# Attention computed by pairs of heads: probabilities divided before they are turned, values as the stationary operand, result produced already transposed

## The chip, the cores and the metric

The kernel runs on one core of a Trainium2 chip. It is one program in which five engines work beside each other: PE (the matrix engine, TensorE), ACT (ScalarE), DVE (VectorE), POOL (GpSimd) and SP (SyncE, which here only issues the weight transfers). They hand work to each other through counters (semaphores). The metric is the device time of one execution in microseconds, the median of several runs; lower is better.

## The reference

Two transformer blocks of two layers each run on one sequence of 256 positions, model width 1024, in fp32. Three of the four layer mixers that matter here are attention, and each is followed by an output projection of width 1024:

```python
# "a": 12 heads of 64, three dilated bands mixed by their log-sum-exps (12*64 + 256 gated columns go into w_out)
scores = einsum(q, k) * dh ** -0.5; scores = where(valid, scores, NEG_INF)
# "c": 8 heads with 96 columns in q and k, 64 in v, and 8 grouped heads of 64 (8 query heads on 2 key heads)
p = softmax(einsum('bqkgc,bskc->bkgqs', q, k) * scale, axis=-1)
out = einsum('bkgqs,bskc->bqkgc', p, v)
# "s": 8 heads of 64 with a relative bias, a causal window and one sink logit per head,
#      beside a depthwise convolution of 31 taps, whose 512 columns form the other half of w_out's input
probs = softmax(concatenate([scores + bias, sink], -1), -1)[..., :-1]
```

Between the mixers lie mixtures of experts and dense feed-forward layers, which take most of the time and which the change does not touch. In "a" the three bands are computed as one softmax, whose mask carries the logarithm of how many bands hold a key.

## The kernel before

T = 256 positions lie in NT = 2 tiles of P = 128 partitions. The three attentions are made by three functions, one for each engine: `attend_pe` (L742), `attend_act` (L775) and `attend_dve` (L795). They walk through the heads in a hand-written software pipeline. For each head:

- PE makes the scores, two matmuls that stream 256 columns each (L751), into bank 4 or 5. The queries are the stationary operand. Heads of 64 columns lie by twos in the upper and lower 64 partitions of `qkA`, `dT` and `qkS` (`half_rows`), so an even and an odd head use different row halves of the array. The heads of 96 columns use 96 rows each.
- DVE scales the scores and adds the mask or bias (L807; L804 where there is none) into `probs`, then takes the row maxima (L809). For "s" two small steps bring in the sink (L814, L816).
- ACT takes the exponential of each of the two query tiles and sums the rows in passing (L784).
- PE turns the four 128x128 blocks by an ordinary fp32 matmul against the identity (L761) into bank 6 or 7, and ACT copies them to `probsT` (L793).
- PE multiplies them by the values, with a `probsT` block as the stationary operand and 64 value columns streaming (L771, four matmuls), into bank 2 or 3. DVE takes reciprocals of the sums (L825) and divides on the way into `cat` (L828).

PE's order for head i is: scores of i, turn of i-2, values of i-3. After the last head, all of `cat` (positions in the partitions) is turned by PE in transpose mode (`turn_pe`, L359, stages "cat_a", "cat_c", "cat_s", four groups each). ACT copies each group to `hT_hi` in the reduced format fp32r (L391), and DVE makes the rest `cat_lo` (L393) (`split_evac`). The output projection (`split_proj_pe`, L556, L576, L582) then multiplies both parts by weights which ACT and DVE have split in the same way (`unit_hi` L451, `unit_lo` L456), one unit of two 128-row blocks at a time. It starts when the first turned group and the first split unit are there.

What stands around the three attentions:

- "a": PE first makes the gating product (L918), and DVE takes it out (L891), before the first head.
- "c": the projections and turns of q and k come before it.
- "s": DVE also has the convolution's taps (L1485), two after each step of the head loop. After the attention the convolution is turned by PE (L1423), normalised by DVE (L1506 to L1519), passed through the silu by ACT (L1455), and turned again.

SP streams the weights through a ring of six 2 MB slots; a slot is loaded again when the engines release it.

## Time and profile before

| | |
|---|---|
| Runs | 1895.82, 1898.30, 1898.87 us; median 1898.3 us |
| Profiled execution, its span | 1897.7 us, mean granted clock of PE 0.898 |
| Busy: PE, ACT, DVE | 1606.0, 594.1, 886.1 us |
| "a": first scores to first matmul of the output projection | 91.15 to 157.46 us |
| "c": the same | 504.86 to 555.23 us |
| "s": the same | 1111.20 to 1164.64 us |

In the profile a row of the timeline is a run of like instructions: its start, how long it lasts, the engine, the line and the operands, and in brackets the idle time before it. An ordinary fp32 matmul has two records in the trace, so "x8" at L751, L761 or L771 is four matmuls; a transpose has one. The granted clock is written as a share of 2.4 GHz: 1.00 is the higher level and 0.50 is 1.2 GHz.

### The profile page before, as it was taken

Reading aid. Unit: us, or ns where it says so; the run is one execution under the profiler, and the core shown is the slowest. Engines: PE = TensorE matmul, PEld = TensorE weight load, DVE = VectorE, ACT = ScalarE, POOL = GpSimd, SP = SyncE. Lnnn points to the kernel's source line nnn. Section 1 sums busy time; section 2 is a strip of 40 time slices with the busy share of each in tenths; the row PEclk is TensorE's granted clock in tenths of the full one; section 3 lists DMA queues with packets and bytes.
Section 4 is the critical chain, followed back from the end, with each engine's and each line's share of the span. In section 5 each row is a group of like instructions: output and inputs, shape, how many; then the busy total and the mean of one; then the engine's idle time right before and its main releaser. Section 6 shows DMA issues by size and latency. Waiting matters only on the chain.

```text
span 1897.7 us, 27096 instructions
## 1 busy us (share of the span) xinstructions
PE 1606.0 (85%) x11040; PEld 1309.3 (69%) x11040; DVE 886.1 (47%) x1503; ACT 594.1 (31%) x952; POOL 25.2 (1%) x32
## 2 busy tenths in 40 slices
PE   7898766657796865659998988999989998879998
PEld 6787533226585422239998667899989997769997
DVE  5534311105763201145555576655565555475555
ACT  4333100004351100033443033443444442443442
POOL 0000000000100000000000000000000000000000
PEclk9858898788897978889999968999999998989999
DMA  9402499998112999995444422355545543345520
GB/s 405 195 0 89 202 426 428 428 428 344 46 45 73 427 429 428 429 407 206 182 177 179 134 89 83 139 182 185 196 166 195 184 178 129 124 170 206 181 89 22
DMA packets 31024, 409.24 MB, mean 216 GB/s; under 512 B 3376, under 2 KB 5424, under 8 KB 6368
## 3 DMA queue, kind: packets, MB, share of 16 engines
q1 hardware_dynamic: 28496, 404.85, 53.9%
q10 hardware_dynamic: 2448, 3.24, 0.6%
q8 instruction: 60, 0.98, 0.2%
q14 instruction: 20, 0.16, 0.0%
HBM read 407.01 MB, written 1.06 MB: 215 GB/s over the span
## 4 chain that ended last, share of the span: by engine, by line
PE 61%; DMA 17%; issue 12%; DVE 6%; ACT 3%; POOL 1%; SPq 0%; DVEq 0%; ACTq 0%; POOLq 0%
DMA ring<-stream 17%; PE bank L1267 7%; PE bank L1271 7%; PE bank L1268 7%; PE bank L1299 6%; PE bank L576 5%; PE bank L1305 3%; PE bank L751 3%; PE bank L761 3%; PE bank L582 2%; PE bank L1095 2%; PE bank L1541 2%; PE bank L771 2%; PE bank L1076 2%; PE bank L556 2%
## 5 line engine op out<-in xcount | busy, mean ns | idle before, releaser
L456 DVE TENSOR_TENSOR unit_lo<-ring,unit_hi 128x1024 fp32r<-128x1024 f32 x324 | 395.5, 1225 | 348.2 <-ACT unit_hi L451 347.9
L451 ACT ACTIVATE unit_hi<-ring 128x1024 fp32r<-128x1024 f32 x324 | 342.3, 1061 | 472.0 <-PE bank L1271 293.9
L1267 PE MATMUL bank<-hT_hi,unit_hi 128*128 128x256 f32 x1408 | 348.4, 286 | 0.4
L1268 PE MATMUL bank<-norm_lo,unit_hi 128*128 128x256 f32 x1408 | 346.6, 281 | 0.0
L1268 PEld LDWEIGHTS bank<-norm_lo,unit_hi 128*128 128x128 f32 x1408 | 266.6, 189 | 3.1
L1267 PEld LDWEIGHTS bank<-hT_hi,unit_hi 128*128 128x128 f32 x1408 | 265.6, 189 | 4.6 <-DVE norm_lo L395 1.4
L1076 PE MATMUL bank<-ring,work 128*32 128x256 f32 x2048 | 150.9, 451 | 90.9 <-DMA ring<-stream 77.7
L1271 PE MATMUL bank<-hT_hi,unit_lo 128*128 128x256 f32 x1408 | 197.6, 282 | 0.0
L1076 PEld LDWEIGHTS bank<-ring,work 128*32 128x32 f32 x2048 | 72.7, 126 | 167.8 <-DMA ring<-stream 100.3
L1271 PEld LDWEIGHTS bank<-hT_hi,unit_lo 128*128 128x128 f32 x1408 | 181.1, 189 | 0.0
L1299 PE MATMUL bank<-unit_hi,act_lo 128*128 128x512 f32 x336 | 132.4, 394 | 0.0
L1299 PE MATMUL bank<-unit_hi,act_hi 128*128 128x512 f32 x336 | 132.0, 393 | 0.0
L1219 DVE TENSOR_TENSOR work<-work,bank 128x128 f32<-128x128 f32 x32 | 9.2, 288 | 211.1 <-ACT work L1148 211.1
L1095 PE MATMUL bank<-ring,work 128*32 128x256 f32 x1024 | 79.2, 461 | 26.6 <-DMA ring<-stream 20.9
L359 PE MATMUL bank<-con,xn 128*128 128x128 f32 (+1 forms) x184 | 39.7, 404 | 61.6 <-ACT xn L678 61.6
L1305 PE MATMUL bank<-unit_lo,act_hi 128*128 128x512 f32 x336 | 90.1, 390 | 0.0
L1148 ACT ACTIVATE work<-bank 128x128 f32<-128x128 f32 x32 | 8.9, 278 | 248.9 <-PE bank L1076 248.9
L359 PEld LDWEIGHTS bank<-con,xn 128*128 128x128 f32 (+1 forms) x184 | 35.4, 214 | 66.3 <-ACT xn L678 56.7
L1095 PEld LDWEIGHTS bank<-ring,work 128*32 128x32 f32 x1024 | 39.2, 127 | 53.8 <-issue 27.0
L576 PE MATMUL bank<-unit_hi,hT_hi 128*128 128x512 f32 (+1 forms) x192 | 73.6, 389 | 1.4 <-ACT unit_hi L451 1.4
L1305 PEld LDWEIGHTS bank<-unit_lo,act_hi 128*128 128x128 f32 x336 | 63.1, 188 | 14.1
L1227 DVE COPY work<-bank 32x256 f32<-32x256 f32 x64 | 27.2, 424 | 97.8 <-PE bank L1095 97.3
(238 smaller groups left out, 2029.6 us busy)
## 6 DMA issues: line engine op xcount, KB each, us to landing
ring<-stream SPq DMA_DIRECT2D x191, 2048.0 KB, 14.4
work<-spread ACTq DMA_DIRECT2D x2, 1024.0 KB, 7.6
par<-params SPq DMA_DIRECT2D x1, 1451.5 KB, 17.5
x<-x_in SPq DMA_DIRECT2D x1, 1024.0 KB, 5.0
out<-x SPq DMA_DIRECT2D x2, 512.0 KB, 2.7
con<-consts SPq DMA_DIRECT2D x1, 640.0 KB, 5.9
cat<-final_rows ACTq DMA_DIRECT2D x1, 512.0 KB, 3.9
work<-final_rows ACTq DMA_DIRECT2D x1, 512.0 KB, 5.1
```

Of the source, the lines that this page charges most:

```text
L359: last = nc.tensor.transpose(bank[g % 4][0:rows, at:at + cols], src, ident)
L451: nc.scalar.activation(high_buf(name, u), raw_unit(name, u), ACT.Copy).then_inc(hi_done, 1)
L456: low = nc.vector.tensor_tensor(low_buf(name, u), raw_unit(name, u), high_buf(name, u).bitcast(F32), ALU.subtract)
L576: nc.tensor.matmul(proj_bank(m, t)[:, 0:width], left[:, 2 * j + kk, t * P:(t + 1) * P], high[:, kk, 0:width], start=(j == 0 and kk == 0 an ...
L751: mm = nc.tensor.matmul(bank[4 + g % 2][:, t * T:(t + 1) * T], q[:, t * P:(t + 1) * P], k, start=True, stop=True)
L1076: mm = nc.tensor.matmul(bank[4 + e % 2][32 * j:32 * j + 32, 0:256], hcur[:, 4 * half + kk, e * CAP:(e + 1) * CAP], w[:, kk, :, j * P:(j + ...
L1095: mm = nc.tensor.matmul(bank[7][32 * i:32 * i + 32, 0:256], actT_e[:, e % 2, j * CAP:(j + 1) * CAP], w[:, j, i * 256:(i + 1) * 256], start ...
L1267: nc.tensor.matmul(out, high[:, k, :], hT_hi[:, k, :], start=(k == 0), stop=False)
L1268: nc.tensor.matmul(out, high[:, k, :], norm_lo[:, k, :], start=False, stop=False)
L1271: mm = nc.tensor.matmul(out, low[:, k, :], hT_hi[:, k, :], start=False, stop=(k == KD - 1))
L1299: nc.tensor.matmul(bank[j][:, :], left[:, f % 2, t * P:(t + 1) * P], unit_hi[:, u % SPLIT, half * 512:(half + 1) * 512], start=(f == 0 and ...
L1305: mm = nc.tensor.matmul(bank[j][:, :], act_hi[:, f % 2, t * P:(t + 1) * P], unit_lo[:, u % SPLIT, half * 512:(half + 1) * 512], start=Fals ...
```

## The change

Heads are handled by twos. The scores of both go out in turn, tile by tile, into two banks. Where there is a mask or bias, DVE adds it and finds the maximum in one instruction for each half head; where there is none it only reads the maximum out of PSUM, and the exponential reads PSUM and scales. DVE divides the probabilities before they are turned. PE turns them in transpose mode, and then the values are the stationary operand (64 columns: the even head writes partitions 0 to 63, the odd one 64 to 127) with 256 turned probabilities streaming. The product is thus the transposed result, which ACT and DVE split straight into `hT_hi` and `cat_lo`. The turns of `cat` fall away, except for the two blocks of gated columns in "a" (group 3, now made right after the first scores, with PE waiting for its evacuation) and the convolution's half in "s". The convolution's turn now waits for all heads. The mask table, the bias and the sink table are prepared to fit.

```diff
+        def scores_pe(pe, name, i):
+            g, heads = PAIR_AT[name] + i, HEADS[name][2 * i:2 * i + 2]
+            ge(pe, probs_done, g - 1)
+            for t in range(NT):
+                for hh, (q, k, *_) in enumerate(heads):
+                    mm = nc.tensor.matmul(score_bank(g, hh)[:, t * T:(t + 1) * T], q[:, t * P:(t + 1) * P], k,
+                                          start=True, stop=True)
+            mm.then_inc(scores_done, 1)
+        def turn_probs_pe(pe, name, i):
+            pe.wait_ge(norm_done, g + 1)
+            for hh in range(2):
+                ge(pe, probsT_done, 2 * g - 1 + hh)
+                for s in range(NT):
                     for t in range(NT):
-                            mm = nc.tensor.matmul(bank[6 + g % 2][:, s * T + t * P:s * T + (t + 1) * P],
-                                                  probs[:, g % 3, t * T + s * P:t * T + (s + 1) * P], ident,
-                                                  start=True, stop=True)
+                        mm = nc.tensor.transpose(bank[hh][:, s * T + t * P:s * T + (t + 1) * P],
+                                                 probs[:, g % 3, hh, t * T + s * P:t * T + (s + 1) * P], ident)
+                mm.then_inc(probs_turned, 1)
+        def weigh_pe(pe, name, i):
+            ge(pe, cat_low, g - 1)
+            for s in range(NT):
+                for hh in range(2):
+                    if s == 0:
+                        pe.wait_ge(probsT_done, 2 * g + hh + 1)
+                    at = hh * NT * T + s * T
+                    mm = nc.tensor.matmul(bank[2 + g % 2][64 * hh:64 * hh + 64, 0:T], heads[hh][2](s),
+                                          PROBS_T[name][:, g % 2, at:at + T], start=(s == 0), stop=(s == NT - 1),
+                                          skip_group_check=True)
+            mm.then_inc(heads_done, 1)
+        def attend_pe(pe, name, between=None):
+            n = PAIRS[name]
+            scores_pe(pe, name, 0)
+            scores_pe(pe, name, 1)
+            if between is not None:
+                between()
+            for i in range(n):
+                if i >= 1 and i + 1 < n:
+                    scores_pe(pe, name, i + 1)
+                turn_probs_pe(pe, name, i)
+                if i >= 1:
+                    weigh_pe(pe, name, i - 1)
+            weigh_pe(pe, name, n - 1)
+        def attend_act(act, name, between=None):
+            for i in range(n):
+                exp_act(act, name, i)
+                if i == 0 and between is not None:
+                    between()
+                if i >= 1:
+                    probsT_act(act, name, i - 1)
                 if i >= 2:
+                    heads_hi_act(act, name, i - 2)
+            probsT_act(act, name, n - 1)
+            heads_hi_act(act, name, n - 2)
+            heads_hi_act(act, name, n - 1)
+        def masked_dve(v, name, i):
+            v.wait_ge(scores_done, g + 1)
+            for hh, head in enumerate(heads):
+                if head[4] is None:
+                    last = nc.vector.tensor_reduce(top[:, 2 * hh:2 * hh + 2],
+                                                   score_bank(g, hh)[:, :].rearrange("p (t s) -> p t s", t=NT), AX.X,
+                                                   ALU.max)
+                    continue
+                for t in range(NT):
+                    last = nc.vector.tensor_tensor_reduce(probs[:, g % 3, hh, t * T:(t + 1) * T],
+                                                          score_bank(g, hh)[:, t * T:(t + 1) * T], head[4](t), head[3], OFF,
+                                                          ALU.add, ALU.max, top[:, c:c + 1])
+        def norm_probs_dve(v, name, i):
+            v.wait_ge(probs_done, g + 1)
+            step(v, nc.vector.reciprocal(rsum, sums))
+            for hh in range(2):
+                for t in range(NT):
+                    last = nc.vector.tensor_scalar(row, row, rsum[:, c:c + 1], None, ALU.mult)
+            last.then_inc(norm_done, 1)
+        def heads_lo_dve(v, name, i):
+            v.wait_ge(cat_hi, g + 1)
+            nc.vector.tensor_tensor(cat_lo[:, i, :], bank[2 + g % 2][:, 0:T], hT_hi[:, i, :].bitcast(F32),
+                                    ALU.subtract).then_inc(cat_low, 1)
+        def attend_dve(v, name, between=None, first=None):
+            masked_dve(v, name, 0)
+            masked_dve(v, name, 1)
+            if first is not None:
+                first()
+            for i in range(n):
+                norm_probs_dve(v, name, i)
+                if i >= 1 and i + 1 < n:
+                    masked_dve(v, name, i + 1)
+                if i >= 2:
+                    heads_lo_dve(v, name, i - 2)
                 if between is not None:
                     between(i)
+            heads_lo_dve(v, name, n - 2)
+            heads_lo_dve(v, name, n - 1)
...
-            attend_dve(v, "a")
+            attend_dve(v, "a", first=lambda: split_evac(v, 1, "cat_a", 3))
-            attend_act(act, "a")
+            attend_act(act, "a", lambda: split_evac(act, 0, "cat_a", 3))
-            attend_pe(pe, "a")
-            pe.wait_ge(turn_src, 2)
-            pe.wait_ge(cat_done, HEAD_AT["a"] + A_HEADS)
-            turn_pe(pe, "cat_a")
+            def gated_turn():
+                pe.wait_ge(turn_src, 2)
+                turn_pe(pe, "cat_a")
+                pe.wait_ge(*TURN_DONE[TURN_AT["cat_a"][0]])
+            attend_pe(pe, "a", gated_turn)
...
             attend_pe(pe, "c")
-            pe.wait_ge(cat_done, HEAD_AT["c"] + C_HEADS + G_HEADS)
-            turn_pe(pe, "cat_c")
...
             attend_pe(pe, "s")
             pe.wait_ge(conv_done, 1)
+            pe.wait_ge(cat_low, PAIR_AT["s"] + PAIRS["s"])
...
-            pe.wait_ge(cat_done, HEAD_AT["s"] + S_HEADS)
-            turn_pe(pe, "cat_s", 0, 2)
             pe.wait_ge(conv_cat, 1)
-            turn_pe(pe, "cat_s", 2, 4)
+            turn_pe(pe, "cat_s")
...
-            attend_dve(v, "s", lambda i: taps(104 + 2 * i, min(106 + 2 * i, 4 * KW)))
+            attend_dve(v, "s", lambda i: taps(104 + 5 * i, 109 + 5 * i))
```

The new ACT functions: `exp_act` waits for the pair's maxima and makes four exponentials of 256 columns (and the sink's for "s"); `probsT_act` copies each head's 512 turned columns as soon as they are there; `heads_hi_act` makes `hT_hi` from 256 columns of the product.

## Rows read from the trace of the kernel before

**Rows 1.** By stretch: busy us of PE, PEld, DVE, ACT, POOL; clock, DMA, GB/s
```profile
130.00:140.00 10.00, 10.00 (x37) 8.09 (x36) 2.39 (x7) 3.15 (x10) 0.00 (x0) 0.50 0.00 0
499.00:502.00 3.00, 3.00 (x15) 2.81 (x15) 1.53 (x6) 0.65 (x2) 0.00 (x0) 0.50 0.03 5
502.00:504.80 2.80, 2.07 (x19) 1.80 (x17) 1.89 (x6) 1.98 (x7) 0.00 (x0) 0.99 0.00 0
523.00:547.00 24.00, 24.00 (x163) 20.35 (x163) 14.14 (x34) 12.72 (x41) 0.00 (x0) 1.00 0.00 1
1120.00:1145.00 25.00, 25.00 (x90) 20.44 (x89) 14.96 (x42) 8.33 (x30) 0.00 (x0) 0.50 0.00 1
```

**Rows 2.** Timeline of PE in "a": start us, us, line, operands, count
```profile
91.15 2.09 PE L751 MATMUL bank<-work 64*128 64x256 f32 x8
...
98.73 2.07 PE L751 MATMUL bank<-work 64*128 64x256 f32 x4
100.73 2.07 PE L761 MATMUL bank<-con,work 128*128 128x128 f32 x8
...
152.48 1.96 PE L771 MATMUL bank<-work 128*128 128x64 f32 x16
...
157.46 0.47 PE L576 MATMUL bank<-unit_hi,hT_hi 128*128 128x512 f32 x1 [0.59 <-ACT unit_hi L451]
```

**Rows 3.** Timeline of PE in "c" and the turns before it
```profile
498.80 3.52 PE L359 MATMUL bank<-con,work 128*96 128x128 f32 x16 [2.81 <-DVE xn L982]
502.16 1.91 PE L359 MATMUL bank<-con,xn 128*96 128x128 f32 x16
504.86 1.97 PE L751 MATMUL bank<-work 96*128 96x256 f32 x8 [0.79 <-DVE work L373]
...
550.38 1.96 PE L771 MATMUL bank<-work 128*128 128x64 f32 x16
...
555.23 0.47 PE L576 MATMUL bank<-unit_hi,hT_hi 128*128 128x512 f32 x1 [0.47 <-ACT unit_hi L451]
```

**Rows 4.** Timeline of PE in "s" and at its projection
```profile
1111.20 2.08 PE L751 MATMUL bank<-work 64*128 64x256 f32 x8 [5.37 <-issue]
...
1151.54 1.96 PE L771 MATMUL bank<-work 128*128 128x64 f32 x16
...
1164.64 0.78 PE L576 MATMUL bank<-unit_hi,hT_hi 128*128 128x512 f32 x1
...
1168.90 0.39 PE L576 MATMUL bank<-unit_hi,hT_hi 128*128 128x512 f32 x1
```

**Rows 5.** DVE's instructions by line and shape: busy, mean ns, idle before
```profile
L393 DVE TENSOR_TENSOR cat_lo<-bank,hT_hi 128x256 fp32r<-128x256 f32 x24 | 9.0, 418 | 2.9 <-ACT hT_hi L391 2.9
L688 DVE CUSTOM_DVE_ANT_0 xn<-x 128x1024 f32<-128x1024 f32 x12 | 14.7, 1225 | 5.0 <-DMA x<-x_in 4.6
L688 DVE DVE_READ_ACCUMULATOR2_ANT stat<- 128x1 f32 x12 | 1.0, 82 | 0.0
L809 DVE TENSOR_REDUCE stat<-work 128x2 f32<-128x512 f32 x36 | 24.7, 686 | 1.2
L1658 DVE TENSOR_SCALAR work<-work,stat 128x256 f32<-128x256 f32 x8 | 2.2, 349 | 17.9 <-ACT work L1594 17.9
L1485 DVE SCALAR_TENSOR_TENSOR cat<-work,par,cat 128x256 f32<-128x256 f32 x120 | 48.6, 478 | 0.0
```

**Rows 6.** Timeline of ACT in "a"
```profile
107.89 0.51 ACT L784 ACTIVATE work<-work,stat 128x256 f32<-128x256 f32 x1 [4.04 <-DVE stat L809]
...
108.40 0.49 ACT L784 ACTIVATE work<-work,stat 128x256 f32<-128x256 f32 x1
...
108.89 0.57 ACT L793 ACTIVATE work<-bank 128x512 f32<-128x512 f32 x1
```

**Rows 7.** ACT's splitting of a weight unit, by line
```profile
L451 ACT ACTIVATE unit_hi<-ring 128x1024 fp32r<-128x1024 f32 x324 | 342.3, 1061 | 472.0 <-PE bank L1271 293.9 <-PE bank L1305 114.4 <-PE bank L582 58.2
```

**Rows 8.** Timeline of PE, an expert's matmuls on 32-column strips of the array
```profile
211.12 3.66 PE L1076 MATMUL bank<-ring,work 128*32 128x256 f32 x64 [1.26 <-issue]
```

More of the change, by code:

```diff
@@ new lines, in build, with pair_stat, score_bank @@
+        PAIRS = {name: len(heads) // 2 for name, heads in HEADS.items()}
+        PAIR_AT = {"a": 0, "c": PAIRS["a"], "s": PAIRS["a"] + PAIRS["c"]}
+        SINK_NEG = 216
+        def pair_stat(g, what):
+            at = 20 * (g % 3) + 4 * ("top", "sums", "sink", "sink_exp", "rsum").index(what)
+            return stat[:, at:at + 4]
+        def score_bank(g, hh):
+            return bank[4 + 2 * (g % 2) + hh]
+        def scores_pe(pe, name, i):
[6 more added lines that the diff above has]
+            mm.then_inc(scores_done, 1)
@@ new lines, in attend_pe, with exp_act @@
+        def attend_pe(pe, name, between=None):
[11 more added lines that the diff above has]
+            weigh_pe(pe, name, n - 1)
+        def exp_act(act, name, i):
+            g, heads = PAIR_AT[name] + i, HEADS[name][2 * i:2 * i + 2]
+            act.wait_ge(masked_done, g + 1)
+            top, sums = pair_stat(g, "top"), pair_stat(g, "sums")
+            for hh, head in enumerate(heads):
+                for t in range(NT):
+                    row, c = probs[:, g % 3, hh, t * T:(t + 1) * T], 2 * hh + t
+                    masked = head[4] is not None
+                    src = row if masked else score_bank(g, hh)[:, t * T:(t + 1) * T]
+                    last = nc.scalar.activation(row, src, ACT.Exp, bias=top[:, c:c + 1], scale=1.0 if masked else head[3],
+                                                accum_out=sums[:, c:c + 1])
+            if name == "s":
+                last = nc.scalar.activation(pair_stat(g, "sink_exp"), pair_stat(g, "sink"), ACT.Exp)
+            last.then_inc(probs_done, 1)
```

172 lines of the change are left out of this document (68 added, 104 removed).

## Prediction

> **What bounds the kernel now.** I read the busy time by stretch first, because the page's averages mix the attention with stages that the change leaves alone. In the middle of each attention PE is busy all the time (10.00 of 10.00 us in "a", 24.00 of 24.00 in "c", 25.00 of 25.00 in "s"), while DVE has 2.4, 14.1 and 15.0 us of work in them and ACT 3.2, 12.7 and 8.3 [rows 1]. So PE sets the pace. It does so at two speeds: the granted clock is 0.50 in "a" and "s" (1.2 GHz) and 1.00 in "c" (2.4 GHz) [rows 1]. No weights move in these stretches (0 or 1 GB/s) [rows 1]: the ring is full, and what the attention saves no transfer takes back. The timelines then give the length of each stage. In "a" the last product ends at 152.48 + 1.96 = 154.44, 63.3 us after the first scores, and the projection starts 3.0 us later [rows 2]. In "c" these are 552.34, 47.5 us and 2.9 us [rows 3]; in "s" 1153.50, 42.3 us and 11.1 us, the last for the convolution's normalising and turns [rows 4].
>
> **PE's work for a pair.** Scores: in "a" the first two heads stood together in PE's queue. Their four matmuls took 2.09 us, and later the two of one head alone 2.07 [rows 2]. So heads in different row halves run at once, and the pair costs 2.1 us at the low clock instead of 4.1, and about 1.1 at the high one. The 96-column heads don't overlap: four matmuls took 1.97 at the high clock [rows 3]; I take 1.85 in a stream, and 3.6 at the low clock. Turns: a head's four matmuls against the identity took 2.07 at the low clock [rows 2], while 16 transposes took 3.52 at the low and 1.91 at the high one [rows 3], 0.22 and 0.12 each. Eight cost 1.95 and 1.1 with their start, instead of about 4.0 and 2.1. Values: before, two heads cost about 1.96 us at the high clock (the rows hold 16 records, so two heads) [rows 2 to 4]. Now there are four matmuls of 256 columns, with 64 stationary columns each, in two halves of the array. The trace has no such shape. The nearest is the experts' 32-column strips: 32 matmuls of 256 columns in 3.66 us, 0.11 each [rows 8], against 0.49 for one alone [rows 3], so four strips run at once. If two halves do the same, the pair costs 1.05 and 1.95 (high, low clock); if not, 1.9 and 3.6. I take the first, as the nearer row. In sum a pair costs PE 3.25 us at the high clock (4.0 with 96 columns) and 6.0 at the low (7.5), where "a" took 63.3/6 = 10.5 and "c" 47.5/8 = 5.9.
>
> **DVE and ACT: a new ring.** DVE divides pair i before it masks pair i+1, ACT can only then exponentiate i+1, and DVE waits for that to divide it. The three steps are in series and become the pace wherever PE is faster.
> - Divide: four multiplications of 256 columns at 2.2/8 = 0.275 [rows 5], with an allowance of 0.3 for the reciprocal and the hand-over inside DVE: 1.4 us.
> - Mask, "a": the fused instruction is only there for 1024 columns, 1225 ns and 82 for reading the maximum [rows 5]. A 256-column subtraction occupies 9.0/24 = 0.375 [rows 5]. So four cost 4 x 0.46 = 1.8 to 1.3 (if it scales by length alone, 4 x 0.39 = 1.55); with 0.2 for the sign I take 1.95. "c" only reads the maximum, 2 x 0.69 [rows 5] and 0.2: 1.55. "s": 2.25 with the sink's steps.
> - Exponentials: 0.50 from one to the next [rows 6]: 2.0 us; 2.1 reading PSUM, 2.2 with the sink.
>
> With 0.05 for each of three hand-overs the ring turns in 5.5 us in "a", 5.2 in "c", and 6.0 in "s", plus what the five taps (5 x 48.6/120 = 2.0 us [rows 5]) stick out behind the exponential, 0.2 to 0.4.
>
> **The three stages.** "a", high clock: the first scores wait for the gating columns to be taken out; masks of pairs 0 and 1 end at 5.2. The group of gated columns is copied by ACT and DVE by 6.8 (two copies of 256 columns each, PE waiting behind it with nothing else to do), pairs 0 and 1 are divided at 9.6 and pair 2 at 16.0, then three turns of the ring at 5.45 give 32.3, and the last transposes and two products 3.2: 35.5 us against 63.3. At the low clock pair 2 is divided at 18.8, PE's 6.0 sets the pace up to 36.8, and the end costs 3 x 1.95: 42.6. I take 38: low at the start as now, then PE has an unbroken row of full-width work and I expect the clock to rise. "c", high clock: scores 1.85, mask to 3.5, exponentials of two pairs to 7.7, pair 1 divided at 9.2; PE has the scores of pair 2 at 10.05, which are masked, exponentiated and divided by 15.25; five turns of 5.15 give 41.0, and the end 3.2: 44.2. At the low clock PE alone needs 4 x 7.5 + 4 x 6.0 = 54, and 4.4 to fill: 58.4. Before it was 47.5. Here the heads were already fast (3.0 us each), so little is won. I take 46, since PE idles 3.4 us while pair 0 is masked, exponentiated and divided, and may lose the clock for a while. "s", high clock: two masks to 5.65, pair 0 divided at 7.3, taps to 9.3, pair 1 divided at 10.8, pair 2 masked, exponentiated and divided at 17.0, one more turn 23.2, the end 3.2: 26.4 against 42.3. The low clock adds 1.5 at the start and 2.7 at the end: 30.6. I take 28.5.
>
> What follows the last product: in "a" and "c" the projection now waits for one copy of 256 columns (0.4, as a subtraction [rows 5]) and the first `unit_hi`, 1.06 [rows 7]: 1.6 us instead of 3.0. The turns of `cat` were in that stretch, and with it they are free. A projection that starts at the low clock loses time: in "s" the first unit took 1168.90 - 1164.64 = 4.3 us, and its first matmul 0.78 where the next unit's took 0.39 [rows 4]. I put the loss at a third of the unit, 1.4, as an estimate, and charge half. In "s" the convolution's turn moves behind the last `cat_low`: copy and subtraction, 0.8 to 1.0 on top of the 11.1.
>
> Sum: "a" 38 + 1.6 + 0.7 - 66.3 = -26.0; "c" 46 + 1.6 + 0.7 - 50.4 = -2.1; "s" 28.5 + 1.0 - 42.3 = -12.8. Together -41. I hold back 2 us for what the walk leaves out (PE's passing between 64-row, whole and 64-column tiles, for which no row gives a price): -39. The profiled 1897.7 becomes 1858.7; the median of the runs is 0.6 higher, so the forecast is 1859 us.
>
> **The rivals.**
> - **The clock stays at 0.50 in all three (20%).** For it: "a" and "s" are at 0.50 for their whole middle although PE never rests [rows 1], and the new PE has pauses. The time: "a" 42.6 + 1.6 + 1.4 - 66.3 = -20.7, "c" 58.4 + 1.6 + 1.4 - 50.4 = +11.0, "s" 30.6 + 1.0 - 42.3 = -10.7, together -20: 1878 us. Against it: transposes alone, at 0.50 from 499 to 502, were followed by 0.99 from 502 on [rows 1]. The Trainium skill ("TensorE: Matmul & The Clock Gate", Part 4: PE-mode transpose) says that transposes don't count as PE being busy for the clock, which speaks for this rival, as a third of PE's work becomes transposes; this trace's 499 to 502 speaks against that rule.
> - **The clock is at 1.00 nearly throughout (15%).** "a" 35.5 + 1.6 - 66.3 = -29.2, "c" -4.6, "s" 26.4 + 1.0 - 42.3 = -14.9: -49, 1849 us.
> - **The ring is slower than its parts (15%).** Steps that wait for each other pay their whole duration: a multiplication is 349 ns, not 275 [rows 5], which is 0.3 us a turn, and I allow as much for the mask and twice that for the exponentials. At 1.2 us more a turn, over some 12 turns, 14 us come back: 1873 us.
> - **The products' halves don't overlap, and the clock is low (5%).** Then PE needs 7.7 us a pair (9.2 with 96 columns). The walk gives 50.9, 70.2 and 35.5, with the same ends -12.4, +22.8 and -5.8: 5 us slower, 1902. It decides where PE's pair is dearer than 5.9 us, the pace of "c" now. The scores' overlap [rows 2] and the strips' [rows 8] speak against it. It is also how the change would fail to do what it says.
>
> **How the numbers follow.** The forecast has 45%, its own range is 1850 to 1868. The range for 8 in 10 reaches from the fast clock case to the slow one: 1846 to 1879. A change of 0.2% (3.8 us), about what a measurement of this kernel can tell from none, is passed by every case but the last: faster 0.92; same 0.03, where the slow cases add up to the old time; slower 0.05.
>
> **What would show it.** In the new profile: records of the scores of a pair beginning together; the product's four matmuls in 1.05 or 1.95 us; ACT's exponentials of successive pairs 5.2 to 6.2 us apart, with DVE's division just before each turn; PE no longer busy throughout at the high clock; the projection 1.6 us behind the last product. I am wrong if PE is still busy throughout "c", or if the fused mask costs much over 0.5 us. Outside the three stages nothing should move, but for a shift of where the clock changes among the experts.

## The result, and the profile after

The changed kernel takes 1841.8 us (1840.0 to 1843.1) where the kernel before took 1897.1 (1893.9 to 1898.9) beside it: a ratio of 0.9721, with a 95% interval from 0.9697 to 0.9745. The forecast was 1859 with a range from 1846 to 1879. So the sign was right, and the size was outside the range: 55 us came off instead of 39. The two profiled spans are 1897.7 and 1838.2 us, 59.5 apart, and where these lie can be read stage by stage. (The profiled execution of the changed kernel is the shortest of its four, so 59.5 is more than the 55.)

| stage (first scores to first projection product, or as named) | before | after | difference | forecast |
|---|---|---|---|---|
| "a" | 66.3 | 39.2 | -27.1 | -26.0 |
| "c" | 50.4 | 44.6 | -5.8 | -2.1 |
| "s" | 53.4 | 40.6 | -12.9 | -12.8 |
| four feed-forward stages (second: 185.8 and 183.2) | | | -2.45, -2.62, -2.30, -2.40 = -9.8 | 0 |
| from L1399 (after: L1491) to L529 (L543), ahead of "s" | 30.1 | 27.7 | -2.4 | 0 |
| all else | | | -1.6 | 0, and +2 held back |

One execution of each kernel lies behind this table. The length of "c" varies with the clock at its end: in three more profiled executions with the changed kernel's instructions, reported below, it took 45.9 to 46.2 us, so -5.8 is the most that "c" gave.

First the busy time by stretch, to be held against [rows 1]. The columns are again the stretch, its length, the busy us of PE, PEld, DVE, ACT and POOL, then the clock.

```profile
104.00:112.00 8.00, 5.97 (x47) 3.68 (x45) 4.34 (x22) 5.01 (x18) 0.00 (x0) 1.00 0.00 0
499.00:515.00 16.00, 10.60 (x82) 7.01 (x84) 10.77 (x32) 10.01 (x35) 0.00 (x0) 1.00 0.01 2
1085.00:1110.00 25.00, 10.89 (x62) 6.33 (x56) 18.64 (x52) 12.66 (x32) 1.01 (x1) 0.68 0.00 0
```

No engine is busy throughout any more. PE, which had no gap in [rows 1], now rests a third of the time in "c", and DVE and ACT are each busy two thirds of it. Engines that are all partly idle beside each other are what a serial loop over several of them looks like. The chain of waits of the changed kernel, from 501 to 506 us in "c", names the loop (start, length, engine and line). This loop is the ring of the prediction, and "a turn of the ring" is one pass through it; PE's turns at L785 are the transposes:

```profile
501.40 1.57 ACT work L827 x7
...
503.00 0.19 DVE stat L895
...
503.21 1.14 DVE work L899 x4
504.35 1.21 DVE stat L869 x2
505.56 0.02 issue
505.58 0.18 DVE stat L885
...
507.75 0.19 DVE stat L895
```

Exponentials (L827), reciprocal (L895), division (L899), maximum (L869), sign (L885), and the exponentials of the next pair again: from the reciprocal at 503.00 to the one at 507.75, the turn is 4.75 us, and TensorE isn't in it. PE's timeline shows the same turn from its side, in "a" first, beside [rows 2]:

```profile
90.89 3.35 PE L773 MATMUL bank<-work 64*128 64x256 f32 x16
...
108.74 1.09 PE L785 MATMUL bank<-con,work 128*128 128x128 f32 x8 [1.94 <-DVE work L899]
109.76 1.08 PE L798 MATMUL bank<-work 128*64 128x256 f32 x8
110.77 1.13 PE L773 MATMUL bank<-work 64*128 64x256 f32 x8
113.81 1.70 PE L785 MATMUL bank<-con,work 128*128 128x128 f32 x8 [1.90 <-DVE work L899]
115.44 1.97 PE L798 MATMUL bank<-work 128*64 128x256 f32 x8
...
123.95 1.61 PE L785 MATMUL bank<-con,work 128*128 128x128 f32 x8 [2.96 <-DVE work L899]
125.49 3.06 PE L798 MATMUL bank<-work 128*64 128x256 f32 x16
130.08 0.47 PE L589 MATMUL bank<-unit_hi,hT_hi 128*128 128x512 f32 x1 [1.52 <-ACT unit_hi L454]
```

The turns L785 start at 108.74, 113.81 and, with one left out, 123.95: 5.07 us each, whether PE's work beside them ran at the high clock (1.09 + 1.08 + 1.13) or in part at the low one (1.70, 1.97). The last product ends at 128.55, 37.7 us after the first scores, and the projection follows 1.5 us later. In "c", beside [rows 3]:

```profile
478.55 3.69 PE L773 MATMUL bank<-work 96*128 96x256 f32 x16 [0.89 <-ACT work L372]
...
486.55 3.41 PE L773 MATMUL bank<-work 96*128 96x256 f32 x8
...
504.40 1.09 PE L785 MATMUL bank<-con,work 128*128 128x128 f32 x8 [1.58 <-DVE work L899]
...
509.16 1.09 PE L785 MATMUL bank<-con,work 128*128 128x128 f32 x8 [1.58 <-DVE work L899]
...
519.69 1.95 PE L798 MATMUL bank<-cat,work 128*64 128x256 f32 x16
523.16 0.47 PE L589 MATMUL bank<-unit_hi,hT_hi 128*128 128x512 f32 x1 [1.52 <-ACT unit_hi L454]
```

and in "s", beside [rows 4], where the convolution's normalising between L1516 and L360 is still the long end:

```profile
1071.46 3.79 PE L773 MATMUL bank<-work 64*128 64x256 f32 x16 [4.66 <-DVE work L374]
...
1096.48 3.68 PE L798 MATMUL bank<-work 128*64 128x256 f32 x16
1101.19 1.06 PE L1516 MATMUL bank<-con,cat 128*128 128x128 f32 x8 [1.04 <-DVE cat_lo L906]
1110.39 1.97 PE L360 MATMUL bank<-con,cat 128*128 128x128 f32 x8 [8.13 <-ACT cat L1546]
1112.01 0.78 PE L589 MATMUL bank<-unit_hi,hT_hi 128*128 128x512 f32 x1
```

The parts of the ring were forecast from [rows 5] and [rows 6]. By line and shape (busy, mean ns, idle before) they are:

```profile
L876 DVE CUSTOM_DVE_ANT_0 work<-bank,con 128x256 f32<-128x256 f32 x24 | 8.7, 419 | 3.7 <-PE bank L773 3.7
L869 DVE TENSOR_REDUCE stat<-bank 128x2 f32<-128x512 f32 x16 | 10.3, 682 | 5.1 <-PE bank L773 5.1
L827 ACT ACTIVATE work<-bank,stat 128x256 f32<-128x256 f32 x32 | 14.7, 475 | 14.9 <-DVE stat L885 14.9
```

What counts in a row of such instructions is their pitch, from one start to the next. The fused mask is 419 ns long, and its pitch is 0.345 us (starts at 108.60, 108.94, 109.29, 109.63). The exponentials from PSUM are 475 ns long and start 0.45 apart (501.03, 501.50, 501.94, 502.39).

### The profile page after: what moved, and what is told of

The parts are those of the page before. It is cut to its first block, busy times and chain, and to the rows that moved or that the text cites. A ratio compares the mean times of both kernels' runs of the same rounds, so it can differ in the third digit from the quotient of the medians.

```text
span 1838.2 us, 26373 instructions
## 1 busy us (share of the span) xinstructions
PE 1513.3 (82%) x10716; PEld 1217.2 (66%) x10716; DVE 871.4 (47%) x1548; ACT 591.2 (32%) x947; POOL 25.3 (1%) x32
## 4 chain that ended last, share of the span: by engine, by line
PE 56%; DMA 17%; issue 12%; DVE 10%; ACT 4%; POOL 1%; SPq 0%; DVEq 0%; ACTq 0%; POOLq 0%
DMA ring<-stream 17%; PE bank L1359 7%; PE bank L1360 7%; PE bank L1363 7%; PE bank L1391 6%; PE bank L589 5%; PE bank L1397 3%; PE bank L595 3%; PE bank L1632 2%; PE bank L1168 2%; PE bank L1187 2%; PE bank L360 2%; PE bank L569 2%; DVE cat L1576 2%; PE bank L1491 2%
## 5 line engine op out<-in xcount | busy, mean ns | idle before, releaser
L1359 PE MATMUL bank<-hT_hi,unit_hi 128*128 128x256 f32 x1408 | 342.7, 282 | 0.1
L1360 PE MATMUL bank<-norm_lo,unit_hi 128*128 128x256 f32 x1408 | 341.6, 280 | 0.0
L1359 PEld LDWEIGHTS bank<-hT_hi,unit_hi 128*128 128x128 f32 x1408 | 266.4, 189 | 3.8 <-DVE norm_lo L398 0.5
L360 PE MATMUL bank<-con,xn 128*128 128x128 f32 (+1 forms) x184 | 39.1, 398 | 61.5 <-ACT xn L692 61.5
L360 PEld LDWEIGHTS bank<-con,xn 128*128 128x128 f32 (+1 forms) x184 | 34.8, 211 | 66.2 <-ACT xn L692 56.7
```

The source lines that it names most:

```text
L360: last = nc.tensor.transpose(bank[g % 4][0:rows, at:at + cols], src, ident)
L1359: nc.tensor.matmul(out, high[:, k, :], hT_hi[:, k, :], start=(k == 0), stop=False)
L1360: nc.tensor.matmul(out, high[:, k, :], norm_lo[:, k, :], start=False, stop=False)
```

## The experiments

Three questions were open. What sets the pace in the changed attentions, the ring or TensorE? What shortened the feed-forward stages, in which no instruction differs? And how much of "a" is less work, how much a faster clock?

### The ring

**Scores and masks two pairs ahead.** PE makes the scores of pair i+2, and DVE masks them, while pair i is divided and turned. In `attend_pe` and `attend_dve`:

```diff
-                if i >= 1 and i + 1 < n:
-                    scores_pe(pe, name, i + 1)
+                if i + 2 < n:
+                    scores_pe(pe, name, i + 2)
...
-                if i >= 1 and i + 1 < n:
-                    masked_dve(v, name, i + 1)
+                if i + 2 < n:
+                    masked_dve(v, name, i + 2)
```

> The changed kernel, with scores and maxima made two pairs ahead and not one: in every turn of the loop TensorE issues the scores of pair i+2 before the turns of pair i, and VectorE divides pair i and then masks pair i+2, so that the exponentials of pair i+1 run beside the division of pair i. Theory 1 (the turn of 5.07 us in the first attention and 4.75 us in the second is a serial ring of division, mask and exponentials over VectorE and ScalarE): a turn falls to the busiest engine alone, 3.6 to 3.9 us (ScalarE: four exponentials of 0.49, two evictions of 0.58, one of 0.37 us; VectorE about the same); that gives 5 turns x 1.2 = 6 us in the first and 7 turns x 1.0 = 7 us in the second attention, 0 to 2 us in the third, where the convolution's taps fill VectorE: 1827 to 1830 us. Theory 2 (TensorE sets the turn, with its clock at 0.5 to 1.0): 0 to -2 us, 1840 to 1842 us.

Measured: 1815.6 us (1810.6 to 1817.4), 0.9582 of the kernel before (0.9516 to 0.9649). That is 26 us under the changed kernel, twice what I expected. "a" took 29.0 us instead of 39.2, "c" 34.6 instead of 44.6, "s" 38.7 instead of 40.6. PE's timeline of this run in "a":

```profile
104.55 1.14 PE L773 MATMUL bank<-work 64*128 64x256 f32 x8
105.61 1.10 PE L785 MATMUL bank<-con,work 128*128 128x128 f32 x8
106.64 1.08 PE L798 MATMUL bank<-work 128*64 128x256 f32 x8
107.65 1.14 PE L773 MATMUL bank<-work 64*128 64x256 f32 x8
```

The turn is now 3.10 us, TensorE's own three groups without a gap. From 480 to 492 us of "c" three engines are nearly full at once:

```profile
480.00:492.00 12.00, 11.84 (x94) 7.75 (x92) 11.35 (x33) 11.62 (x43) 0.00 (x0) 1.00 0.01 3
```

So the serial ring is shown; theory 2 falls. My 3.6 to 3.9 us was too much because I had summed mean durations, where the pitch counts (0.45 or 0.49 for an exponential, 0.48 to 0.52 for a copy).

**More work in the ring.** In `norm_probs_dve`, ahead of the division, with `extra` a buffer of 512 columns:

```diff
             step(v, nc.vector.reciprocal(rsum, sums))
+            for hh in range(2):
+                step(v, nc.vector.tensor_scalar(extra[:, :], probs[:, g % 3, hh, :], 1.0, None, ALU.mult))
```

> The changed kernel, with two more multiplications of 512 columns on VectorE ahead of each pair's division, into a spare buffer that nothing reads, each waited for: some 1.2 us of VectorE more in each of the 18 turns. Theory 1 (serial ring): each turn of the first and second attention is longer by all of it, 14 x 1.2 = 17 us, and the third by 4 x 1.2 = 5 us at most, as VectorE is full there: 1859 to 1865 us. Theory 2 (TensorE sets the turn): only the first turns of each attention show it, 1 to 4 us: 1843 to 1846 us.

Measured: 1857.1 us (1855.3 to 1859.3), 15.3 more than the changed kernel; "a" 44.6 (+5.5), "c" 53.5 (+8.9), "s" 42.5 (+2.0). DVE's timeline in "c":

```profile
509.78 0.18 DVE L896 RECIPROCAL stat<-stat 128x4 f32<-128x4 f32 x1 [1.67 <-ACT work L828]
509.99 0.89 DVE L898 TENSOR_SCALAR extra<-work 128x512 f32<-128x512 f32 x2
...
515.45 0.18 DVE L896 RECIPROCAL stat<-stat 128x4 f32<-128x4 f32 x1 [1.67 <-ACT work L828]
```

The two steps cost 0.92 us and not 1.2, and the turn went from 4.75 to 5.67: all of it came through. 14 x 0.92 = 12.9 us against 14.4 measured in "a" and "c". A serial ring again.

**Turns as ordinary products**, with the ring and without it. In `turn_probs_pe`:

```diff
-                        mm = nc.tensor.transpose(bank[hh][:, s * T + t * P:s * T + (t + 1) * P],
-                                                 probs[:, g % 3, hh, t * T + s * P:t * T + (s + 1) * P], ident)
+                        mm = nc.tensor.matmul(bank[hh][:, s * T + t * P:s * T + (t + 1) * P],
+                                              probs[:, g % 3, hh, t * T + s * P:t * T + (s + 1) * P], ident,
+                                              start=True, stop=True)
```

On the changed kernel:

> The changed kernel, with the probabilities turned by ordinary products with the identity, as the kernel before did, and not in transpose mode; all else stays. Theory 1 (a serial ring of VectorE and ScalarE sets the turn, TensorE has slack in it): the eight turns of a pair go from 1.1 to some 2.1 us at the high clock, hidden but for the last pair of each attention and the stretches at half clock: 3 x 1 us at the ends and 2 to 4 us in the low stretches, 1845 to 1850 us. Theory 2 (TensorE sets the turn): all 18 pairs show it, 18 x 1 = 18 us at least, 1860 us and more. By the Trainium skill (TensorE: Matmul & The Clock Gate, Part 4: PE-mode transpose) transposes don't count as activity for the clock; by that rule ordinary products would hold the clock up and pay part of their price back, -1 to -4 us against theory 1.

Measured: 1842.1 us (1841.2 to 1846.1), against 1841.8. PE in "c":

```profile
500.20 2.05 PE L785 MATMUL bank<-con,work 128*128 128x128 f32 x16 [0.62 <-DVE work L900]
...
504.95 2.05 PE L785 MATMUL bank<-con,work 128*128 128x128 f32 x16 [0.62 <-DVE work L900]
```

The turns did double, 1.09 to 2.05, and PE's idle time before them fell from 1.58 to 0.62: the ring's 4.75 us stayed and hid them. "c" was 1.9 us longer (at its ends, where nothing covers PE: its first turns took 3.37 us at the low clock, and its last 2.05), "a" 0.5, "s" 0.1 shorter. So **in the changed kernel, transpose mode is worth nothing that can be measured in the whole time.** The granted clock was higher with the ordinary products, 0.88 against 0.78 from 90 to 130 us and 0.82 against 0.62 from 1070 to 1112, which pays part of their price back; but PE was also busier there (28.7 against 26.7 of 40 us), so this doesn't say whether transposes as such count for less.

With scores two pairs ahead:

> Scores two pairs ahead, and the turns as ordinary products. In the changed kernel this cost nothing, since a ring over VectorE and ScalarE hid it. Theory 1 (with scores two pairs ahead TensorE is the bound at 3.1 us a pair, so that its work shows): the turns' 2.05 against 1.09 us make a turn 4.05 us; six and eight turns of the first two attentions, 14 x 0.95 = 13 us, and 1 to 2 us in the third: 1829 to 1831 us. Theory 2 (VectorE or ScalarE sets the turn there too): 1816 to 1819 us.

Measured: 1828.6 us (1824.5 to 1831.3), 13.0 more than with transposes; "a" 33.5, "c" 40.8, "s" 39.3. PE's turn is 4.06 us:

```profile
493.19 1.14 PE L773 MATMUL bank<-work 64*128 64x256 f32 x8
494.26 2.05 PE L785 MATMUL bank<-con,work 128*128 128x128 f32 x16
...
497.25 1.14 PE L773 MATMUL bank<-work 64*128 64x256 f32 x8
```

The same edit costs 0.3 us where a ring covers it and 13 us where nothing does.

**The halves one after the other**, with scores two pairs ahead: the two loops of `scores_pe` are exchanged, and so are those of `weigh_pe` (`for hh` outside).

> Scores two pairs ahead, where TensorE sets the turn of 3.1 us; here the scores and the value products of a pair are issued head by head, and no longer alternating between the two 64-row or 64-column halves of the array. Theory 1 (products on the two halves overlap because they stand next to each other): the eight score products go from 1.13 to some 2 us in the 15 pairs with 64-row heads, the eight value products from 1.08 to some 2 us in all 18; a turn rises from 3.1 to 4.5 to 5 us, 1815.6 + 20 to 28 = 1836 to 1844 us. Theory 2 (a product of 64 rows or columns is short by itself, or the order makes no difference): 3.1 us stay, 1815.6 us.

Measured: 1817.7 us (1816.5 to 1818.9), 2.1 more, and within the spread of the run without the exchange (1810.6 to 1817.4). PE's groups in "c":

```profile
483.20 1.14 PE L773 MATMUL bank<-work 64*128 64x256 f32 x8
...
485.44 1.09 PE L798 MATMUL bank<-cat,work 128*64 128x256 f32 x8
```

So theory 1 is wrong where it says that the halves overlap because they stand next to each other. The groups kept their length, and their records still start in pairs, 13 ns apart instead of 7, which I read as one for each half. The row halves do overlap: in the kernel before, the four records of one head alone took as long as the eight of two (2.07 and 2.09 us, [rows 2]). But they don't need to alternate in the program. For the column halves the pairs of records say the same; no run has one column half alone.

### The feed-forward stages

The changed kernel's larger `sinks` puts the constants and the work buffer 32 bytes further on. That was the only difference that I could find for these stages, so it was made alone, on the kernel before:

```diff
+        pad = sb("pad", [P, 8])
         con = sb("con", [P, NCONST])
```

> The kernel before, with 8 unused columns (32 bytes) put ahead of the constants, so that the constants and the work buffer lie 32 bytes further on, as they do in the changed kernel; no instruction differs. Theory 1 (the four feed-forward stages are shorter in the changed kernel because of where the work buffer lies, whose starting address goes from 32 to 0 modulo 64 bytes): each of the four feed-forward stages, from its first product to the last, is 2.2 to 2.6 us shorter than before, about 9.7 us in sum, and nothing else moves: 1887 us. Theory 2 (it comes from the new program around them: where its instructions lie, or in which phase the clock reaches the stage): the stages keep their length within 0.3 us, 1897 us.

Measured: 1885.5 us, 0.9931 of the kernel before (0.9894 to 0.9968). In the profiled run the feed-forward stages fell by 2.4, 2.6, 2.2 and 2.4 us, within 0.1 of what the change had done to each, 9.6 in sum. Here is the second of them, by PE's timeline: its first product (L1267, L1268 or L1359) and the first of its closing products (L1289, L1290, L1381), in the kernel before

```profile
1196.27 0.56 PE L1267 MATMUL bank<-hT_hi,unit_hi 128*128 128x256 f32 x1
...
1382.09 0.39 PE L1289 MATMUL bank<-unit_hi,act_hi 128*128 128x512 f32 x1
```

in the kernel before with the shift

```profile
1190.04 0.56 PE L1268 MATMUL bank<-hT_hi,unit_hi 128*128 128x256 f32 x1
...
1373.31 0.39 PE L1290 MATMUL bank<-unit_hi,act_hi 128*128 128x512 f32 x1
```

and in the changed kernel

```profile
1143.20 0.56 PE L1359 MATMUL bank<-hT_hi,unit_hi 128*128 128x256 f32 x1
...
1326.41 0.39 PE L1381 MATMUL bank<-unit_hi,act_hi 128*128 128x512 f32 x1
```

They are 185.8, 183.3 and 183.2 us apart. The products of 256 columns start 0.118 us apart after the shift, and 0.116 to 0.125 before it. So this cause is shown, and with it 9.8 us of the 59.5: **they have nothing to do with the attention.**

The shift also took 2.4 us off the stretch ahead of "s", where the kernel before had the clock at 0.91 and this run at 0.99 to 1.00, with the same work. That is the clock alone: the run with the hidden activations shifted, below, lost the same 2.4 us there although its feed-forward stages grew.

What in the address counts? The next nine runs bear on it; the lengths are those of the second feed-forward stage, and the others agree within 0.5 us.

> The kernel before, with only the two buffers of split feed-forward weights (high and low parts) put 32 bytes further on, where they lie in the changed kernel; activations, identity and everything else keep their addresses. Theory 1 (the products are shorter because of where the weights that TensorE loads lie): the four feed-forward stages are 2.2 to 2.6 us shorter each, about -9.7 us, 1887 us. Theory 2 (it is the activations, the identity or another buffer that moved with them): the stages keep their 185.6 to 185.8 us, 1897 us.

`unit_hi` and `unit_lo` alone, 8 columns on: 183.9 us, so 1.7 to 2.0 of the 2.2 to 2.6 are the weights' place; 1884.8 us in all, 0.9904 (0.9861 to 0.9948).

> The kernel before, with every buffer 32 bytes further on, so that all keep their distances from each other. Theory 1 (what counts is where the work buffer lies by itself): the feed-forward stages fall from 185.7 to 183.2 us, as with the work buffer alone shifted. Theory 2 (what counts is its distance from the activations' buffers, which TensorE reads at the same time): they stay at 185.7 us.

The same pad ahead of the first buffer: 185.6 to 185.8 us, each stage within 0.03 of the kernel before; 1897.3 us in all, 1.0021 (0.9990 to 1.0052). So with this shift of 32 bytes it isn't any buffer's place by itself that counts, but the distance between buffers.

> The kernel before, with only the two small buffers of the hidden activations (high and low parts) 32 bytes further on. The weights' buffers alone gave 1.7 of the 2.4 us a stage. Theory 1 (the hidden activations give the rest): 185.7 - 0.7 = 185.0 us a stage. Theory 2 (the rest belongs to another buffer, or to both together): 185.7 us.

`act_hi` and `act_lo` alone: 186.2 us, 0.4 longer; 1896.3 us in all, 1.0001 (0.9986 to 1.0016). Both theories miss: moved alone they cost time, while moving the whole work buffer, these two with it, gives more than moving the weights alone (183.3 us against 183.9).

> The kernel before, with only the buffer of the weights' low parts 32 bytes further on; it feeds one product in three. Theory 1 (each product is shorter by where its own weights lie): a third of the 1.7 us, 185.1 us a stage. Theory 2 (the distance between high and low parts counts): anything else, 185.7 us or the full 183.9 us.

`unit_lo` alone: 184.9 us, 0.7 to 0.9 shorter, some four tenths of the weights' part, and nearer to the third of theory 1 than to either value of theory 2; 1892.1 us in all, 0.9945 (0.9882 to 1.0008).

> The changed kernel, with 8 unused columns ahead of the constants, so that the work buffer again starts at 32 modulo 64 bytes. Theory 1 (address): the four feed-forward stages are each 2.2 to 2.6 us longer than in the changed kernel, 1841.8 + 9.7 = 1851.5 us. Theory 2 (the program around them): no difference, 1841.8 us within 2 us.

The pad on the changed kernel, 64 bytes beyond the kernel before: 181.8 to 182.2 us and 1837.7 us in all. Opposite to theory 1: what counts is not the place modulo 64 bytes.

> The changed kernel, with only the two buffers of split feed-forward weights 32 bytes further on, where they lay in the run with the whole work buffer shifted. Theory 1 (the weights' place): the stages take 181.8 to 182.2 us, as in that run, against 183.2 us, 1841.8 - 5.5 = 1836 us. Theory 2 (another buffer): they stay at 183.2 us, 1842 us.

The weights alone at that place: 182.7 us, between the two theories; 1841.2 us in all.

> The changed kernel, with 24 unused columns (96 bytes) ahead of the constants, so that the work buffer lies 128 bytes beyond its place in the kernel before. Theory 1 (what counts is the place modulo 128 bytes): the feed-forward stages return to 185.6 us, 1841.8 + 9.7 = 1851 us. Theory 2 (what counts is how far the work buffer lies from others): they are at or below the 181.8 us of the shift by 32 bytes, 1836 us or less.

128 bytes beyond the kernel before: 183.9 us, neither the 185.7 of theory 1 nor the 181.8 of theory 2; 1840.0 us.

> Scores two pairs ahead, and the work buffer 192 bytes beyond its place in the kernel before. The stages took 185.7 us at 0, 183.2 at 32, 181.9 at 64 and 183.9 at 128 bytes. Theory 1 (a pattern that repeats after 128 bytes, with the 185.7 us at 0 as its exception): 181.9 us as at 64, 1810.5 us. Theory 2 (64 bytes is a minimum, and the stages grow with the distance beyond it): 184 us or more, 1819 us or more.

192 bytes beyond, with scores two pairs ahead: 183.7 us; 1817.4 us in all. No repetition after 128 bytes, and no steady growth either.

> Scores two pairs ahead, and the work buffer 64 bytes beyond its place in the kernel before (32 beyond the changed kernel's). Theory 1 (the place of the work buffer and the order of the pairs act apart): the feed-forward stages take 181.8 to 182.2 us as they did at this place with the changed kernel, 1815.6 - 5 = 1810.5 us. Theory 2 (the stages' length hangs on the program before them): they stay near 183.2 us, 1815.6 us.

64 bytes beyond, with scores two pairs ahead: 181.8 us as before, so that place and order act apart. This has the lowest median here, **1813.7 us** (1813.0 to 1814.7), 0.9574 of the kernel before (0.9529 to 0.9619) and 28 us under the changed kernel; its gain over the version without the pad, 1.9 us, lies within that one's spread (1810.6 to 1817.4) and is smaller than the stages' 6, since the stage ahead of "s" lost 2.4 of it to the clock.

By distance: 185.7 us at 0, 183.2 at 32, 181.8 at 64, 183.9 at 128 and 183.7 at 192 bytes. Why these and not others, I can't say; it stays open. The Trainium skill (TensorE: Matmul & The Clock Gate, Part 2: What happens when you issue a matmul) says that loading the next weights takes no SBUF read bandwidth from the running product. These stages, in which every product has new weights, depend on how far the weights lie from the other operands (183.9 us against 185.8 with the weights alone moved), which that rule doesn't account for. Whether PE's weight loads meet its streamed operand there, or meet what ACT and DVE read and write beside it, no run tells apart.

### The clock in "a"

The run with only `unit_lo` shifted had something else in it. Its attention is the kernel before's, instruction by instruction and at the same addresses, and yet "a" took 45.1 us there instead of 66.3. By stretch, in the kernel before and then in that run:

```profile
104.00:130.00 26.00, 26.00 (x92) 21.23 (x92) 8.35 (x19) 6.29 (x20) 0.00 (x0) 0.50 0.00 1
```

```profile
104.00:130.00 26.00, 25.76 (x177) 21.99 (x177) 14.28 (x34) 13.11 (x41) 0.00 (x0) 1.00 0.00 1
```

PE did 177 records instead of 92 in the same 26 us, because it was granted 2.4 GHz instead of 1.2. From the first scores up to 104 us both ran at 0.50. A head takes 2.98 us at the high clock and 5.61 at the low one, from one head's turns to the next:

```profile
111.94 2.08 PE L761 MATMUL bank<-con,work 128*128 128x128 f32 x8
...
117.55 2.07 PE L761 MATMUL bank<-con,work 128*128 128x128 f32 x8
```

So the old order can run at either clock from there on. The kernel before takes 1875 to 1901 us from one execution to the next, while the four of the changed kernel lie within 4 us. That its fast ones had a high clock in "a" is likely (those under 1886 us show a mean clock of 0.905 to 0.910, most others 0.897 to 0.904), but the profile of none of them is on record.

That splits the 27.1 us of "a". 21.2 are what the clock alone gave the old order, and from 45.1 to 39.2 us, 5.9, is what the new order gained on the old one at the high clock (with its own "a" still partly low). The new order gets the better clock more often: five profiled executions with the old order (the kernel before and four of the shifted ones) took 65.9 to 66.9 us in "a" and one took 45.1, while all four with the new order took 37.6 to 39.2. What in the new order raises the clock no run shows.

**One part alone: transposes in the kernel before.** In its `attend_pe`, the same exchange of `matmul` with the identity for `transpose`:

> The kernel before, with one part of the change alone: the probabilities are turned in transpose mode; heads stay single, the division stays behind the value products, and the result is still turned at the end. In the kernel before, the turns of a head take 2.07 us at the low and 1.00 at the high clock, of 5.2 and 2.99 for the head. Theory 1 (TensorE sets the pace there, so half of that is saved): 12 heads x 1.05 = 12.6 us in the first attention and 8 x 1.05 = 8.4 in the third, at the low clock; 16 x 0.5 = 8 us in the second, at the high one; 29 us in sum, 1868 us. If the clock rises in the first attention as well, its heads take 2.5 us and it is 20 us shorter still at most. Theory 2 (transposes don't hold the clock up, as the Trainium skill says in TensorE: Matmul & The Clock Gate, Part 4: PE-mode transpose): the second attention falls to the half clock, where a head takes 4.1 us instead of 2.99, 16 x 1.1 = 18 us longer: 1895 us. Theory 3 (the turns lie beside other work): no change.

Measured: 1883.7 us (1881.2 to 1890.9), 0.9972 of the kernel before, with an interval from 0.9935 to 1.0009, so over the whole time it can't be told from it. In the profiled run "a" took 58.9 us (-7.4), "c" 50.0 (-0.4), "s" 50.3 (-3.2).

```profile
113.50 1.11 PE L761 MATMUL bank<-con,work 128*128 128x128 f32 x4
...
118.15 1.11 PE L761 MATMUL bank<-con,work 128*128 128x128 f32 x4
```

A head's turns fell from 2.07 [rows 2] to 1.11 us, and the head from 5.61 to 4.65, by just as much: PE did set the pace of the old order. (The 5.2 us of the expectation was the stage divided by its heads.) That is theory 1, but with 11 us in the three stages and not 29, because the ends of "a" and "c" lost the clock. In "a", twelve heads at 0.96 would be 11.5 us; but the kernel before had 1.00 from 150.5 us on, and made its last products and the turns of `cat` in 1.96 and 1.94 us, where this run had 0.50 until 149.8 and took 3.52 and 3.65. In "c" the clock was 0.91 from 504 to 548 us where it had been 1.00, and that took back nearly all that the shorter turns had gained (in the middle a head took 2.64 us instead of 2.98). So here, as in the changed kernel with and without transposes above (0.78 against 0.88), transposes went with a lower clock, and both times PE also had less work. The Trainium skill (TensorE: Matmul & The Clock Gate, Part 4: PE-mode transpose) says that the full clock doesn't engage for transposes, since they don't count as busy in the same way. This trace agrees in part: the clock fell at the end of "c" (0.61 from 538 to 549 us) but not to 0.50 throughout, and from 104 to 140 us it was 0.50 with either form.

## Why the prediction was right or wrong

- **"PE sets the pace" before, a ring after: right.** Before, a head became shorter by what its turns did. After, PE's gaps, the chain, and the runs two pairs ahead and with more work in the ring all show it. In "a" the forecast was 38 us to the end of the products, and 37.7 came; in "s" 28.5, and 28.7 came. Both forecasts were values chosen between a walk at the high and one at the low clock (35.5 and 42.6, 26.4 and 30.6), and in "a" misses cancelled in part: against the high walk pair 2 was divided after 17.9 us and not 16.0, three turns of the ring took 15.2 and not 16.4, and the end took 4.6 and not 3.2. So how near they came is partly luck.
- **"Outside the three stages nothing should move": wrong, and the largest miss.** The prediction put this term at nothing, and it was 9.8 us in the feed-forward stages; without them the time would have been 1841.8 + 9.8 = 1851.6 us, inside the range. 2.4 more ahead of "s" are the clock. I had read the diff for instructions and not for addresses: `("sinks", 8)` to `("sinks", 16)` stood in it, and moved every buffer behind the parameters against those ahead of them. The run with only that shift shows it. No view of the profile of before could have priced it.
- **"c" was mis-sized, -2.1 instead of -5.8.** Three terms. The turn of 5.15 was 4.75, 2.0 us over five turns, because the exponentials from PSUM had a pitch of 0.45 and not 0.525, and reading the maximum 0.6 and not 0.69. For a lower clock I had put 1.8 us on the 44.2 of my own walk at the high clock; the clock did fall after PE had idled 3.2 us, but only for a short while (0.56 from 486.5 to 490 us, where the scores of pair 2 took 3.41), and pair 2 was divided 16.4 us after the first scores and not 15.25, which is 1.1. And the projection started at the full clock, where I had charged 0.7. The result, 43.1 us to the last product, lies 1.1 under that walk. In the three other executions named at the table, the last products ran at the low clock in part, and "c" was 1.3 to 1.6 us longer: they would still be 2 us under the forecast.
- **The ring's parts in "a": 5.45 forecast, 5.07 came.** The fused mask has a pitch of 0.345 where I took 0.44, a value between 0.39 (the 1024-column row by its length) and 0.46 (a subtraction of 256 columns and the reading) [rows 5]. With the pitch of the multiplications from L1658, 0.275, I had been right (0.265, and four in 1.14 with the last one's tail).
- **The 2 us held back** for TensorE's passing between tile shapes were not needed: the three groups follow each other without a gap in 3.10 us.
- **Values in two column halves: right**, 1.08 us at the high and 1.97 at the low clock, forecast 1.05 and 1.95. So the rival that would have made it slower had no ground.
- **The rival "clock at 1.00 nearly throughout" was the nearest in time, and not in mechanism**: 1849 us, with 15%. The clock was 0.79 over "a", 0.96 over "c" and 0.63 over "s", which is mixed in two of three; the addresses, which it didn't have either, brought the time near it. With the 9.8 us of the addresses taken off, its 1849 would have become 1839, and the forecast's 1859 would have become 1849. The rival "clock stays at 0.50" fell in "a" and "c"; in "s" the clock was mostly low and 1.00 from 1084 to 1090 us. The Trainium skill's rule on transposes (TensorE: Matmul & The Clock Gate, Part 4: PE-mode transpose) had spoken for it. A third of PE's work in "c" is transposes, and "c" ran at 0.96, with its transposes from 490 us on in 1.09 us for eight, against 1.97 at the low clock.
- **The rival "ring slower than its parts" fell the other way.** Steps that wait for each other inside one engine cost their pitch, and only the last of a group its whole duration.
- **What is left of the miss.** Between the forecast's 39 us and the 59.5 of the profiled spans lie 9.8 (addresses), 3.7 ("c"), 2.4 (clock ahead of "s"), 2.0 (held back), 1.1 ("a"), 0.1 ("s") and 1.6 spread over the rest, which no run explains.
- **What the forecast didn't say: how much of "a" was the clock.** Its sum had the old 66.3 us in it as if they were a property of the old order. The old order takes 45.1 us when the clock rises at 104 us.

## What to carry to other kernels

When engines are all partly idle, follow the chain once round, time one turn, and look for a step that can be issued one item earlier: here, making scores and masks two pairs ahead on two engines took 26 us more off, nearly half of what the whole change had brought. Read a diff for sizes of buffers as well as for instructions, and give a changed layout its own run before any reason is built on the stages that it moves. Before crediting an order with a stage's gain, look at the granted clock on both sides of the comparison.

## What the runs showed of the hardware

- The distance between SBUF buffers changes the pitch of TensorE's products: 185.7 us a stage at one distance, 181.8 at another 64 bytes on, the same to 0.03 us when all buffers move together by 32 bytes. I had expected nothing from 32 bytes.
- Products on different row or column halves overlap even where the program issues them half by half: four of 256 columns took 1.14 and 1.09 us at the high clock, and 1.14 and 1.08 where the program alternates.
- Turning by a transpose takes near half of what an ordinary product with the identity takes: 1.09 against 2.05 us for eight blocks at the high clock, 1.11 against 2.07 for four at the low one.
- The same instructions of the first attention held 0.50 up to 150 of its 157 us in one execution and had 1.00 from 104 us on in another, with PE busy 26.0 and 25.8 of 26 us.
- A fused mask and maximum of 256 columns from PSUM has a pitch of 0.345 us; a multiplication of 512 columns from SBUF to SBUF has one of 0.46 with its wait (two in 0.92), less than two of 256 columns (0.265 each).
